# Memory attention: queries straight behind the mix on unnormalised x, values behind them, the heads' attention between these units

## The reference

```python
def rms_norm(x, g):
    y = x * lax.rsqrt(jnp.mean(x * x, axis=-1, keepdims=True) + 1e-6)
    return y * g

# in second_block, layer l: h is (1, 256, 1024), mem is (1, 256, 1024)
mem_n = rms_norm(mem, norm_mem_g[l])
h = h + memory_cross_attention(rms_norm(h, norm_xattn_g[l]), mem_n, w_xq[l], w_xkv[l], w_xo[l])

def memory_cross_attention(h, mem_n, w_xq, w_xkv, w_xo):   # 4 heads of 256
    q = (h @ w_xq).reshape(bsz, seq, 4, 256)
    k, v = jnp.split(mem_n @ w_xkv, 2, axis=-1)
    s = jnp.einsum("bshd,bmhd->bhsm", q, k) * (256 ** -0.5)
    pr = jax.nn.softmax(s, axis=-1)
    o = jnp.einsum("bhsm,bmhd->bshd", pr, v).reshape(bsz, seq, 1024)
    return o @ w_xo
```

## Time and profile before

| | |
|---|---|
| runs | 2196.33 us median, 2196.2 to 2198.81 |
| profiled execution, its own time | 2199.28 us |
| its span, first to last instruction | 2197.5 us |
| busy: TensorE, VectorE, ScalarE | 2107.7, 1653.7, 1075.3 us |
| mean granted TensorE clock | 0.988 of full speed |

### The profile page before, as it was taken

How to read it: one execution, slowest core, us unless ns; L and a number is a source line. 1 busy time by engine, 2 the same in 40 slices (tenths; PEclk the granted TensorE clock), 3 DMA queues, 4 the chain that set the end, 5 groups by cost and what they waited for, 6 DMA issues and landing times.

```text
span 2197.5 us, 40176 instructions
## 1 busy us (share of the span) xinstructions
PE 2107.7 (96%) x16382; PEld 2039.2 (93%) x16382; DVE 1653.7 (75%) x2444; ACT 1075.3 (49%) x1307; POOL 240.0 (11%) x168
## 2 busy tenths in 40 slices
PE   8999999999999999999999989999999999989997
PEld 7888999999989999989999879999988999879997
DVE  7877798778769877898965658767698976648765
ACT  6766344346754434355435445444346435445442
POOL 0001045100005500002202000100001301000100
PEclk9999999999999999999999999999999999999999
DMA  6544455454235455444544424445444544424543
GB/s 249 176 159 147 142 185 189 149 201 163 105 115 176 164 192 191 159 168 154 192 155 171 173 93 176 173 157 206 174 173 152 192 173 170 157 95 173 175 157 109
DMA packets 57847, 361.61 MB, mean 165 GB/s; under 512 B 6688, under 2 KB 9312, under 8 KB 20576
## 3 DMA queue, kind: packets, MB, share of 16 engines
q1 hardware_dynamic: 57696, 359.48, 46.0%
HBM read 358.37 MB, written 1.08 MB: 164 GB/s over the span
## 4 chain that ended last, share of the span: by engine, by line
PE 87%; DVE 6%; ACT 3%; issue 3%; POOL 1%; DMA 0%; SPq 0%; DVEq 0%; ACTq 0%; POOLq 0%
PE acc L615 73%; PE acc L614 6%; ACT w_hi L1907 3%; DVE w_lo L1095 2%; PE pA L710 1%; PE pA L965 0%; PE acc L903 0%; PE pA L1038 0%; PE pB L1038 0%; POOL in_lo L2479 0%; PE pB L989 0%; PE pD L1049 0%; PE pC L1049 0%; PE pA L717 0%; PE pC L755 0%
## 5 line engine op out<-in xcount | busy, mean ns | idle before, releaser
L615 PE MATMUL acc<-in_hi,w_hi 128*128 128x256 f32 x4784 | 1348.8, 287 | 46.1 <-issue 18.6
L615 PE MATMUL acc<-in_hi,w_lo 128*128 128x256 f32 x4784 | 1335.4, 284 | 0.0
L615 PE MATMUL acc<-in_lo,w_hi 128*128 128x256 f32 x4784 | 1272.6, 284 | 2.9 <-POOL in_lo L2479 2.9
L1095 DVE TENSOR_TENSOR w_lo<-raw,w_hi 128x2048 fp32r<-128x2048 f32 (+1 forms) x349 | 757.7, 2171 | 309.9 <-ACT w_hi L1907 308.6
L1907 ACT CAST w_hi<-raw 128x2048 fp32r<-128x2048 f32 (+1 forms) x349 | 630.5, 1807 | 732.7 <-PE acc L615 677.2
L615 PEld LDWEIGHTS acc<-in_hi,w_hi 128*128 128x128 f32 x4784 | 923.9, 193 | 55.7 <-issue 27.6
L615 PEld LDWEIGHTS acc<-in_hi,w_lo 128*128 128x128 f32 x4784 | 923.1, 193 | 0.2
L615 PEld LDWEIGHTS acc<-in_lo,w_hi 128*128 128x128 f32 x4784 | 885.3, 193 | 4.7 <-POOL in_lo L2479 3.4
L2479 POOL TENSOR_TENSOR in_lo<-arena,in_hi 128x256 f32 (+2 forms) x112 | 145.2, 1296 | 1275.3 <-ACT in_hi L2351 523.4
L1720 DVE SCALAR_TENSOR_TENSOR arena<-arena,cols 128x256 f32<-128x256 f32 x480 | 200.4, 491 | 0.0
L2189 ACT CAST in_hi<-arena 128x256 f32 (+1 forms) x88 | 35.8, 407 | 185.3 <-POOL arena L2489 99.0
(11 more groups left out here) (268 smaller groups left out, 1435.1 us busy)
## 6 DMA issues: line engine op xcount, KB each, us to landing
raw<-in_wide SPq DMA_DIRECT2D x285, 1024.0 KB, 4.8
raw<-in_narrow SPq DMA_DIRECT2D x64, 704.0 KB, 4.0
arena<-cs_rows SPq DMA_DIRECT2D x16, 256.0 KB, 5.8
arena<-in_mem SPq DMA_DIRECT2D x3, 1024.0 KB, 6.9
x<-in_x SPq DMA_DIRECT2D x4, 256.0 KB, 6.6
raw<-in_wide SPq DMA_DIRECT2D x2, 512.0 KB, 6.4
tables<-in_tables SPq DMA_DIRECT2D x1, 1024.0 KB, 14.2
arena<-cs_rows SPq DMA_DIRECT2D x16, 64.0 KB, 5.9
```

The lines of the kernel that those rows point to most:

```text
L615: return mm(outs[m], w[:, k, at], moving[:, c, :], start=start, stop=stop)
L1095: tt(w_lo[g % 2][:, 0:n], raw[g % RAW][:, 0:n], w_hi[g % 2][:, 0:n], ALU.subtract).then_inc(lo_ready, 1)
```

## The change

It is in the memory stage, the residual of the mix ahead of it, and the order of two projections.

- mem_q comes ahead of mem_v, in the list of segments and in the weights.
- `residual("mix")` makes early parts for x_norm. All four query units take them. The statistics' product is inside the first (no `wide_tail`). The eight normalised chunks and their parts are gone.
- VectorE takes the queries out of PSUM (`x_query`), scaled by `rstd` and by 1/16, in place of ScalarE's copies.
- Scores, maxima, exponentials, scalings and transpositions go by head, both halves of the tokens together. They stand between the units of mem_q and mem_v: on TensorE behind a unit, on VectorE and ScalarE in the round of a unit, behind its split.
- mem_o's first two units are done in parts of two or more chunks, heads 2 and 3's outputs between them, with `some_chunks`, which is `some` of the attention stage made general.
- Early units of a later norm count on in `early_v` by `scaled_units`, as the mem_q units aren't scaled in PSUM; the numbers of the norms shift by one per layer.

```diff
-        s += [("mem_v", ...MEM_AT), ("mem_q", ...XN_AT), ("mem_o", ...)]
+        s += [("mem_q", ...XN_AT), ("mem_v", ...MEM_AT), ("mem_o", ...)]
 # TensorE
+            def some_chunks(seg, u, ks, back, high, low):
+                g = seg.base + u
+                if ks[0] == 0:
+                    pe.wait_ge(hi_ready, g + 1)
+                    pe.wait_ge(lo_ready, g + 1)
+                    pe.wait_ge(acc_free, g - back)
+                pe.wait_ge(inh_ready, high)
+                pe.wait_ge(in_ready, low)
+                for m in range(2):
+                    for k in ks:
+                        ...three matmuls...
             def x_scores(l, h):
+                pe.wait_ge(acc_free, [s.base for s in segs if s.name == "mem_q"][l] + h + 1)
+                if h >= 2:
+                    pe.wait_ge(xexp_a, XH * l + h - 1)
+                for t in range(TT):
+                    for c in range(2):
+                        last = mm((pA, pB)[h % 2][:, t * T:(t + 1) * T], ...)
                 last.then_inc(xsc_mm, 1)
+            def x_turn(l, h):
+                pe.wait_ge(xpn_v, XH * l + h + 1)
+                if XH * l + h:
+                    pe.wait_ge(xpt_a, XH * l + h)
+                for t in range(TT):
+                    for s in range(TT):
+                        last = transpose(pC[...], x_p[:, h % 2, t, s * P:(s + 1) * P], ident[:])
+                last.then_inc(xpt_mm, 1)
             def cross(l):
+                    def queries(u, j):
+                        if j >= 2:
+                            x_scores(l, j - 2)
+                        if j >= 3:
+                            x_turn(l, j - 3)
+                    def values(u, j):
+                        if j < 2:
+                            x_scores(l, j + 2)
+                        if j < 3:
+                            x_turn(l, j + 1)
+                        if j == 2:
+                            x_out(l, 0)
+                            x_out(l, 1)
+                    project("mem_q", after=queries, early=4 + 3 * l, early_at=XN_AT, stats=norm_stats)
+                    project("mem_v", after=values)
+                    some(0, (0, 1, 2, 3))
+                    x_out(l, 2)
+                    x_out(l, 3)
+                    some(0, (4, 5))
+                    some(1, (0, 1))
+                    some(0, (6, 7))
+                    some(1, (2, 3, 4, 5, 6, 7))
+                    for u in range(2, seg.units):
+                        unit(u, u)
 # VectorE
-                    residual("mix")
+                    residual("mix", 4 + 3 * l, f"x_norm{l}", XN_AT)
+            def x_query(l, seg, u):
+                dve.wait_ge(unit_done, seg.base + u + 1)
+                stt(out=x_q[:, 2 * u:2 * u + 2, :], in0=acc[...], scalar=XHD ** -0.5,
+                    in1=rstd[...], op0=ALU.mult, op1=ALU.mult).then_inc(acc_free, 1)
+            def x_scaled(l, h):
+                dve.wait_ge(xexp_a, XH * l + h + 1)
+                E.mark(recip(small[...], small[...]))
+                E.settle()
+                E.mark(ts(x_p[:, b, 0, :], ...))
+                ts(x_p[:, b, 1, :], ...).then_inc(xpn_v, 1)
             def cross(l):
+                    reciprocal_std(rstd[:])
+                    for u in range(4):
+                        x_query(l, q, u)
+                        split(u + 2, q, u + 2)
+                        if u == 3:
+                            x_scaled(l, 0)
+                        if u >= 2:
+                            x_max(l, u - 2)
+                    for u in range(4):
+                        split(u + 2, v, u + 2)
+                        if u < 3:
+                            x_scaled(l, u + 1)
+                        if u < 2:
+                            x_max(l, u + 2)
+                        if u == 2:
+                            x_low(l, 0)
+                            x_low(l, 1)
+                    x_low(l, 2)
+                    x_low(l, 3)
 # ScalarE
             def cross(l):
+                    norm_root()
+                    for u in range(4):
+                        split(u + 2, q, u + 2)
+                        if u >= 2:
+                            x_exp(l, u - 2)
+                        if u == 3:
+                            x_turned(l, 0)
+                    for u in range(4):
+                        if u == 3:
+                            ...the values' second pair is copied out...
+                        split(u + 2, v, u + 2)
+                        if u == 1:
+                            ...the values' first pair is copied out...
+                        if u < 2:
+                            x_exp(l, u + 2)
+                        if u < 3:
+                            x_turned(l, u + 1)
+                        if u == 2:
+                            x_high(l, 0)
+                            x_high(l, 1)
+                    x_high(l, 2)
+                    x_high(l, 3)
```

More of the change, by code:

```diff
@@ L83, in segments @@
               ("mix", "feat", DC, 4, MIX_AT)]
-        s += [("mem_v", "tok_pair", DC // 2, 4, MEM_AT), ("mem_q", "feat", DC, 4, XN_AT), ("mem_o", "feat", DC, 4, HEADS_AT)]
+        s += [("mem_q", "feat", DC, 4, XN_AT), ("mem_v", "tok_pair", DC // 2, 4, MEM_AT), ("mem_o", "feat", DC, 4, HEADS_AT)]
         s += [("up_b", "feat", DC, FC, 0), ("down", "pair", FC // 2, 16, DC)]
@@ L921, in attention, with some @@
                 seg, unit, _ = units("att_o")
[L923 to L940, removed]
+                def some(u, ks):
+                    some_chunks(seg, u, ks, 1, piece["heads"][0] + ks[-1] + 1, made["heads"][0] + ks[-1] + 1)
                 att_scores(6)
@@ L994, in run @@
                     E.passed(in_ready, NORM_PIECES)
-                    project("glu", needs=parts("norm", 3 + 3 * l, NORM_PIECES, DC // NORM_PIECES, in_ready),
-                            early=3 + 2 * l, stats=norm_stats if l else two_norm_stats)
+                    project("glu", needs=parts("norm", 3 + 2 * l, NORM_PIECES, DC // NORM_PIECES, in_ready),
+                            early=3 + 3 * l, stats=norm_stats if l else two_norm_stats)
                     project("ret_q")
@@ L1054, in run @@
                 def run():
[L1055 to L1071, removed]
@@ new lines, in run, with some @@
+                    project("mem_q", after=queries, early=4 + 3 * l, early_at=XN_AT, stats=norm_stats)
+                    project("mem_v", after=values)
+                    seg, unit, _ = units("mem_o")
+                    def some(u, ks):
+                        some_chunks(seg, u, ks, 3, piece["xheads"][l] + ks[-1] // 2 + 1, made["xheads"][l] + ks[-1] // 2 + 1)
+                    some(0, (0, 1, 2, 3))
+                    x_out(l, 2)
+                    x_out(l, 3)
+                    some(0, (4, 5))
@@ L1569, in second @@
                         tt(f_h[:, j % 2, :], f_s[:, j % 2, :], banks[0], ALU.mult).then_inc(acc_free, 1)
-                    project("up_b", first, second, steps={v_order: 2, silu_ready: 1}, early=True, nth=4 + 2 * l, behind=8)
+                    project("up_b", first, second, steps={v_order: 2, silu_ready: 1}, early=True, nth=5 + 3 * l, behind=8)
                     E.passed(inh_ready, FC)
                     if l + 1 < LAYERS2:
-                        residual("down", 5 + 2 * l, f"mix_norm{l + 1}", 0)
+                        residual("down", 6 + 3 * l, f"mix_norm{l + 1}", 0)
                     else:
@@ L1862, in run @@
[L1862 to L1875, removed]
@@ L1876, in run @@
-                    x_low(XH - 1)
-                    residual("mem_o", 4 + 2 * l, f"f_norm{l}", LATE_AT)
+                    q = take("mem_q")
+                    reciprocal_std(rstd[:])
[6 more added lines that the diff above has]
+                            x_max(l, u - 2)
+                    v = take("mem_v")
@@ new lines, in run @@
+                    for u in range(4):
[9 more added lines that the diff above has]
+                    x_low(l, 3)
+                    E.passed(inh_ready, XH)
+                    residual("mem_o", 5 + 3 * l, f"f_norm{l}", LATE_AT)
@@ L2429, in run @@
-                    v_base = [s.base for s in segs if s.name == "mem_v"][l]
-                    v_out = wide_out(v_base, x_v)
-                    def values(u, j, banks):
-                        v_out(u, j, banks)
-                        if j == 0:
-                            norm_root()
-                        if j == 1:
-                            high_parts(xn, XN_AT, NORM_PIECES, DC // NORM_PIECES, val_ready)
-                    project("mem_v", values)
-                    project("mem_q", copy_out(chunk_of(x_q)), steps={a_order: 1})
@@ L2517, in _ @@
             stages(mamba, ffn("up_a", 0), lambda: skip("att_k", "att_v", "att_q", "att_o"),
-                   ffn("up_a", 1), second=lambda l: (mixer(l), lambda: skip("mem_v", "mem_q", "mem_o"),
+                   ffn("up_a", 1), second=lambda l: (mixer(l), lambda: skip("mem_q", "mem_v", "mem_o"),
```

133 lines of the change are left out of this document (72 added, 61 removed).

## The result

The changed kernel takes 2215.21 us, median of 5 runs (2212.62 to 2219.01), against 2196.33 (2196.2 to 2201.59): ratio 1.0078, 95% interval 1.0062 to 1.0095, some 17 us slower. The profiled execution took 2213.1 us (span 2211.3), that of before 2199.3.

The account below looks back on a forecast made before the run. TensorE, busy 96% of the span, was taken as the bound. Per stage 84.5 + 2.5 + 15.3 + 0.2 = 102.5 us, +5.8 over both layers, plus 9 for the clock, gave +15 (rounded): 2211 us, range 2199 to 2222.

Parts of the forecast that it names:

- TensorE's own work: Memory stage: TensorE's matmuls and transposes take 84.5 us per layer, before and after alike.
- (a): Mix residual: its new early parts, 1.5 us per unit, run beside TensorE's units and cost nothing.
- (b): First query unit: TensorE waits 2.5 us per layer for the sums of the statistics' product.
- (c): Turns of the probabilities: TensorE waits for scalings queued behind the split, 3 × 3.4 + 5.1 = 15.3 us per layer.
- (d): Query units: VectorE's x_query replaces ScalarE's copies, about 0.8 us of VectorE per round, cost 0.
- (f): DMA: the order of mem_q and mem_v in the stream changes, not its size; cost nothing.
- (e): mem_o begun in parts: TensorE waits 0.2 us ahead of its third unit.
- Sum at full clock: Memory stage without clock falls: 102.5 us per layer against 98.8 and 100.4, together +5.8 us.
- The clock: Low clock after the stages' ten waits: seven of ten at 1.3 us each, +9 us; all ten in full, +17.
- Total: Whole kernel: +5.8 + 9 = +15 us (rounded), 2214 us for the profiled execution, 2211 for the median.
- the prediction's count of places of 1.9 us or longer: Kernel before, mid-kernel: eight TensorE standstills of 1.9 us or longer in one piece, six followed by low clock.
- hidden: Rival, chance 0.09: turns find their probabilities ready, stages take 87.0 us, −25 us, 2171 us.

Follow-up runs that it names:

- experiment 4: Changed kernel with VectorE's scaling ahead of the split in all four rounds, and the wide tail for the first query unit's statistics: 2167.37 us, ratio 0.9872.
- experiment 1: Changed kernel with VectorE's scaling of the probabilities ahead of the split in all four rounds: 2172.72 us, ratio 0.9895.
- experiment 5: Changed kernel with the outputs of heads 0 and 1 ahead of turn 3 on TensorE: 2205.16 us, ratio 1.0022.
- experiment 6: Changed kernel with TensorE's turn of each head one unit later, VectorE's order untouched: 2171.94 us, ratio 0.9876.
- experiment 3: Changed kernel with unread matmuls ahead of the turns, 20 for each of turns 0 to 2 and 36 for turn 3: 2205.23 us, ratio 1.0030.
- experiment 9: Changed kernel with the wide tail alone for the first query unit's statistics: 2209.78 us, ratio 1.0054.
- experiment 2: Changed kernel with VectorE's scaling ahead of the split for turn 3 alone: 2196.31 us, ratio 0.9996.
- experiment 8: The kernel of experiment 4 again, unchanged, in more rounds: 2167.31 us, ratio 0.9857 to the kernel before.

## Why the prediction was right

It gave 2211 us and slower; measured were 2215.2. Point by point:

- *TensorE's own work, 84.5 us per stage.* Held: in experiment 4 the stage is 85.3, of which 0.42 is the statistics' wait and 0.30 that ahead of mem_o's third unit.
- *(a) Early parts beside the mix cost nothing.* Held: the mix's units follow each other at 5.76 us in the changed kernel as in the one before.
- *(b) Statistics, 2.5 us.* Measured 2.33, in both layers.
- *(c) The turns, 3 × 3.4 + 5.1 = 15.3 us.* Measured 3 × 3.37 + 5.10 = 15.2, in both layers, by the waits of the list. By the distance from turn to turn they cost somewhat more, 15.9, as the sum below shows. Experiments 1, 5 and 6 show the mechanism from three sides: VectorE's order, TensorE's filling, TensorE's place of the turn.
- *(d) and (f), nothing.* Held: in layer 0 of the changed kernel TensorE's rows show no wait but the statistics', the four turns' and that of (e).
- *(e) 0.2 us.* Measured 0.30, in the changed kernel and in experiment 4.
- *Sum at full clock, 102.5 us.* The measured parts give 103.2. Layer 0 of experiment 1 has no low clock and no wait at the turns and takes 87.24 us. What the waits add is read from turn to turn, at full clock: 11.21 us in the changed kernel against 7.67 in experiment 1, so 3.54 for each of three, and 11.24 against 5.92 for the last, so 5.32. That makes 15.94, and 87.24 + 15.94 = 103.2. Experiment 3 agrees: its stages of 104.9 and 104.7 have one fall of the clock each, 3.4 us low, and half of that taken off leaves 103.2 and 103.0.

First two turns of the changed kernel, layer 1, then four of experiment 1, layer 0, TensorE in order of time:

```profile
1929.52 0.66 PE L1057 MATMUL pC<-ident,arena 128*128 128x128 f32 x4 [3.37 <-DVE arena L1896]
1940.73 0.66 PE L1057 MATMUL pC<-ident,arena 128*128 128x128 f32 x4 [3.37 <-DVE arena L1896]
...
1246.33 0.60 PE L1057 MATMUL pC<-ident,arena 128*128 128x128 f32 x4
1254.00 0.60 PE L1057 MATMUL pC<-ident,arena 128*128 128x128 f32 x4
1261.66 0.60 PE L1057 MATMUL pC<-ident,arena 128*128 128x128 f32 x4
1267.58 0.60 PE L1057 MATMUL pC<-ident,arena 128*128 128x128 f32 x4
```

- *The clock, +9 us.* This term was mis-sized. The stages took 109.6 and 110.8, so 6.4 and 7.6 us went beyond 103.2, 14.0 in all. The count of this trace was the forecast's, seven of ten waits were followed by low clock, and not all ten, the other case it priced. That it fits exactly is luck: it was six of ten in experiment 5, five of eight in experiment 9 and three of eight in experiment 2. What failed is the size: three of the seven falls lasted 6.8 us and not 3.4 (1257 to 1266, 1281 to 1290 and 1965 to 1974). Together TensorE was at 1.2 GHz for 34.1 us of the stages. The forecast also let too much of that lie inside the waits: only 4.7 us did, ahead of three of the turns. The cost per fall was 2.0 us, not 1.3.
- *Total.* Stages +21 us where +15 stood. By the ratio the whole kernel lost 17, with a 95% interval of 14 to 21. That the profiled execution came out at 2213.1, so near the 2214 forecast for it, is luck: the 7.4 us that it gained outside the stages hid that the clock term was too small.

The trace of before could have shown the longer falls. The prediction took 3.4 us from one place, but the slices from 1197 to 1206 hold 6.8 us of low clock, as do those from 210 to 222:

```profile
1197.00:1200.00 3.00, 1.52 (x12) 1.32 (x11) 1.64 (x2) 0.00 (x0) 2.49 (x1) 0.82 0.16 27
1200.00:1203.00 3.00, 3.00 (x16) 3.00 (x16) 0.00 (x0) 0.00 (x0) 0.00 (x0) 0.50 0.77 322
1203.00:1206.00 3.00, 3.00 (x17) 3.00 (x17) 0.50 (x2) 0.45 (x1) 0.00 (x0) 0.55 0.00 0
```

There TensorE had stood still 1.13 and 1.48 us, two waits that the prediction's count of places of 1.9 us or longer leaves out. Nor were there two drops in the stages of before, but three, 10.3 us of low clock: the third, from 1947 to 1956, follows turns with waits of 1.17 us. So short waits close together were followed by low clock as well.

The Trainium skill, "TensorE: Matmul & The Clock Gate", section "Terms", puts the penalty at the throttled time times (1 − K/N), half of it at half clock. By that rule 34.1 us of low clock cost 17.1, an estimate. The traces give less, 14.0 us: of the low time 4.7 us lay in waits, where it costs nothing, and half of the other 29.4 is 14.7.

What stays open is which wait draws a long fall and which a short one or none. Waits of the same 3.37 us did each of these.

The rival "hidden" was wrong for this change, but its price was right: it named 87.0 us per stage and 2171 us, and experiments 1 and 6, in which the turns are hidden, gave 87.2 to 89.0 and 2172 to 2173. The change's idea holds a gain of 23 us by the ratio of experiment 1, and of 28 to 31 with the wide tail (experiments 4 and 8). The order of two statements turned it into a loss.

## What to carry to other kernels

When work is put "between the units" on several engines, follow one item through every queue and ask, for each engine, what stands in front of it in the same round and what that waits for: if anything in front waits for the unit just done, the item comes a full cast and subtraction late, however little the engines have to do. Put the small step that others wait for ahead of the large one that only refills a buffer, or use its result a unit later. And price a standstill of TensorE above its length: here seven of ten waits of 2.3 to 5.1 us cost 2.0 us each on top.

## What the runs showed of the hardware

Matmuls with nobody to read them made a kernel faster: 96 more per layer, placed in waits, took the ratio from 1.0078 to 1.0030, by keeping the granted clock at 0.98 in place of 0.92. Executions of the same code can also differ by 7 us through where the clock falls. Outside the stages the changed kernel and experiment 3 are alike, and their profiled executions took 1990.9 and 1998.0 us there, with 24.2 and 39.0 us of low clock; half of that difference is 7.4.
